# Squared tiles of two norms added in pairs by accumulating transfers, in a streaming encoder step on one core

## The reference

```
def _rmsnorm(x, g):
    y = x32 * rsqrt(mean(x32 * x32, axis=-1) + EPS) * g
def _swiglu(u, w_in, w_out):
    h = u @ w_in;  a, b = h[..., :D_FF], h[..., D_FF:]
    return (silu(a) * b) @ w_out
...
x = x + 0.5 * _swiglu(_rmsnorm(x, norm_ffn1[i]), ...)
x = x + mixer(_rmsnorm(x, norm_mix[i]))
x = x + 0.5 * _swiglu(_rmsnorm(x, norm_ffn2[i]), ...)
```

## Time and profile before

| what | value |
|---|---|
| time, median of 3 runs | 1911.73 us (1911.7 to 1914.8) |
| the profiled execution: own time | 1912.83 us |
| its span | 1911.0 us |
| TensorE busy | 1879.5 us, 98% |
| VectorE, ACT, POOL busy | 66%, 45%, 18% |
| share of the DMA engines' span: q1, q0 | 28.4%, 22.4% |

### The profile page before, as it was taken

One profiled execution on the slowest core, in us unless ns is written; L12 is line 12 of the kernel. 1 busy time (PEld: TensorE's weight loads), 2 busy tenths in 40 slices (PEclk: granted clock), 3 DMA queues, 4 the chain that ended last, 5 costly groups with the idle time before them and its releaser, 6 DMA issues.

```text
span 1911.0 us, 34429 instructions
## 1 busy us (share of the span) xinstructions
PE 1879.5 (98%) x13850; PEld 1856.6 (97%) x13850; DVE 1262.6 (66%) x1997; ACT 864.2 (45%) x1510; POOL 344.1 (18%) x361
## 2 busy tenths in 40 slices
PE   7999999998999999999999999999999999999998
PEld 7999999998999999999999999999989999999998
DVE  7884488667884488678853885462546988448843
ACT  6552355346652355345532553232434555235532
POOL 2220122121220122132201221200001522012112
PEclk9999999999999999999999999999999999999999
DMA  7763576433763577347644763222113476347632
GB/s 193 168 146 104 122 166 146 112 86 81 171 146 103 123 163 151 107 103 163 147 127 109 165 134 100 88 95 67 56 45 105 102 172 152 106 116 167 132 92 80
DMA packets 116830, 234.71 MB, mean 123 GB/s; under 512 B 13184, under 2 KB 15248, under 8 KB 116672
## 3 DMA queue, kind: packets, MB, share of 16 engines
q1 hardware_dynamic: 77440, 160.59, 28.4%
q0 software_dynamic: 38208, 69.42, 22.4%
q10 hardware_dynamic: 1024, 2.49, 0.3%
HBM read 228.92 MB, written 3.53 MB: 122 GB/s over the span
## 4 chain that ended last, share of the span: by engine, by line
PE 91%; DVE 4%; ACT 2%; DMA 2%; issue 1%; POOL 0%; DVEq 0%; ACTq 0%
PE ps L1774 48%; PE ps L1764 39%; DMA raw_y<-in_ffn_in 1%; DVE u L1234 1%; DVE w_lo L1180 1%; ACT w_hi L706 1%; PE ps L2086 0%; PE ps L2147 0%; PE ps L2089 0%; PE ps L1956 0%; PE ps L2076 0%; DMA x<-in_x 0%; ACT u L748 0%; PE ps L2061 0%; PE ps L2050 0%
## 5 line engine op out<-in xcount | busy, mean ns | idle before, releaser
L1774 PE MATMUL ps<-u,w_hi 128*128 128x288 f32 x4928 | 993.7, 297 | 18.1 <-DVE w_lo L1180 5.5
L1774 PEld LDWEIGHTS ps<-u,w_hi 128*128 128x128 f32 x4928 | 796.2, 189 | 23.6 <-DVE w_lo L1180 13.0
L1774 PE MATMUL ps<-u,w_lo 128*128 128x288 f32 x2464 | 730.9, 297 | 0.0
L1774 PEld LDWEIGHTS ps<-u,w_lo 128*128 128x128 f32 x2464 | 465.4, 189 | 0.0
L1764 PE MATMUL ps<-h_hi,w_hi 128*128 128x288 f32 x1386 | 298.0, 296 | 0.0
L1764 PE MATMUL ps<-h_hi,w_lo 128*128 128x288 f32 x1386 | 298.0, 296 | 0.0
L1764 PE MATMUL ps<-h_lo,w_hi 128*128 128x288 f32 x1386 | 297.9, 296 | 0.0
L706 ACT ACTIVATE w_hi<-w_raw 128x768 fp32r<-128x768 f32 (+3 forms) x164 | 136.0, 837 | 327.4 <-PE ps L1764 255.3
L1180 DVE TENSOR_TENSOR w_lo<-w_raw,w_hi 128x768 fp32r<-128x768 f32 (+3 forms) x164 | 168.7, 1037 | 165.4 <-ACT w_hi L706 163.2
L1764 PEld LDWEIGHTS ps<-h_hi,w_lo 128*128 128x128 f32 x1386 | 223.1, 189 | 0.0
L1764 PEld LDWEIGHTS ps<-h_hi,w_hi 128*128 128x128 f32 x1386 | 222.9, 189 | 0.0
(11 more groups left out here) (258 smaller groups left out, 2143.5 us busy)
## 6 DMA issues: line engine op xcount, KB each, us to landing
raw_a<-in_ffn_in SPq DMA_DIRECT2D x132, 256.0 KB, 3.8
w_raw<-in_ffn_out SPq DMA_DIRECT2D x64, 384.0 KB, 3.2
raw_y<-in_ffn_in SPq DMA_DIRECT2D x88, 256.0 KB, 3.5
raw_x<-in_ffn_in SPq DMA_DIRECT2D x88, 256.0 KB, 2.7
raw_x<-in_ffn_in POOLq DMA_DIRECT2D x88, 256.0 KB, 6.2
raw_y<-in_ffn_in POOLq DMA_DIRECT2D x88, 256.0 KB, 4.9
raw_z<-in_ffn_in POOLq DMA_DIRECT2D x88, 256.0 KB, 4.9
w_raw<-in_ffn_out SPq DMA_DIRECT2D x64, 320.0 KB, 3.0
```

The source lines that it names most:

```text
L1774: mm = pe.matmul(dst, w, m, start=prod in ("M1", "M2", "M5") and kp == 0 and p == 0, stop=kp == KP - 1 and p == 2, skip_group_check=prod i ...
```

## The change

ACT squares all eight tiles as before. Behind it, POOL issues transfers from SBUF to SBUF that add one squared tile of 288 KB to another within `sq8`, and TensorE multiplies the sums. In FFN a three sums are made (2 on 0, 3 on 1, 7 on 5) and tiles 0, 4, 6, 1, 5 are multiplied; in FFN b four sums (1 on 0, 3 on 2, 5 on 4, 7 on 6) and tiles 0, 2, 4, 6. In FFN a three tiles stand ahead of the group of M6, in FFN b two behind the second step of M1. In both, the last two tiles stand behind the last step of M6 instead of one behind each step. TensorE waits for a semaphore of each sum. POOL issues the last two sums of an FFN between `add_s4` of pair 1 and `add_s1` of pair 3.

```diff
+    sq8_summed = [sem(f"sq8_summed{s}") for s in range(4)]
...
+            def sum_squares(f, s, count):
+                to, of = ((0, 2), (1, 3), (5, 7))[s] if f is ffn_a else ((0, 1), (2, 3), (4, 5), (6, 7))[s]
+                pool.wait_ge(sq8_made, DT * f.i + count)
+                pool.dma_start(sq8[:, to, :], sq8[:, of, :], accum_op=ALU.add).then_inc(sq8_summed[s], 16)
...
                 add_s4(f, ph, 1)
+                if ph == 0 and f is ffn_a:
+                    sum_squares(f, 1, 6)
+                    sum_squares(f, 2, 8)
+                elif ph == 0 and f is ffn_b:
+                    sum_squares(f, 2, 6)
+                    sum_squares(f, 3, 8)
                 add_s1(f, ph, 3)
...
             add_s3_first(ffn_a, 0)
+            sum_squares(ffn_a, 0, 2)
...
             add_s3_first(ffn_b, 0)
+            sum_squares(ffn_b, 0, 2)
+            sum_squares(ffn_b, 1, 4)
...
             def norm_tiles(f, turns):
+                tiles = (0, 4, 6, 1, 5) if f is ffn_a else (0, 2, 4, 6)
                 for i in turns:
-                    j = (0, 2, 4, 6, 1, 3, 5, 7)[i] if f is ffn_a else i
-                    pe.wait_ge(sq8_made, DT * f.i + i + 1)
+                    if f is ffn_a and i in (1, 2):
+                        pe.wait_ge(sq8_made, i + 2)
+                    elif f is ffn_a:
+                        pe.wait_ge(sq8_summed[max(0, i - 2)], 16)
+                    else:
+                        pe.wait_ge(sq8_summed[i], 16 * (2 if i < 3 else 1))
...
-                            norm_tiles(f, range(4))
+                            norm_tiles(f, range(3))
...
-                        if order is COLD and products[0] == ("M6", 0):
-                            norm_tiles(f, (4 + kp,))
+                        if order is COLD and products[0] == ("M6", 0) and kp == KP - 1:
+                            norm_tiles(f, (3, 4) if f is ffn_a else (2, 3))
...
                             pe.wait_ge(x_ready, 2 * DT + 6)
-                            norm_tiles(f, range(4))
+                            norm_tiles(f, range(2))
```

More of the change, by code:

```diff
@@ L1813, in norm_tiles @@
             def norm_tiles(f, turns):
+                tiles = (0, 4, 6, 1, 5) if f is ffn_a else (0, 2, 4, 6)
                 for i in turns:
-                    j = (0, 2, 4, 6, 1, 3, 5, 7)[i] if f is ffn_a else i
-                    pe.wait_ge(sq8_made, DT * f.i + i + 1)
+                    if f is ffn_a and i in (1, 2):
[4 more added lines that the diff above has]
+                        pe.wait_ge(sq8_summed[i], 16 * (2 if i < 3 else 1))
+                    last = i == len(tiles) - 1
                     for h in range(2):
-                        mm = pe.matmul(ps[:, 6 + h, 0:HALF], mean_w[:, :], sq8[:, j, h * HALF:(h + 1) * HALF],
-                                       start=i == 0, stop=i == DT - 1, skip_group_check=True)
-                    if i == DT - 1:
+                        mm = pe.matmul(ps[:, 6 + h, 0:HALF], mean_w[:, :], sq8[:, tiles[i], h * HALF:(h + 1) * HALF],
+                                       start=i == 0, stop=last, skip_group_check=True)
+                    if last:
                         mm.then_inc(norm_psum, 1)
```

## The result

The changed kernel takes 1919.37 us (median of 14 runs), the kernel before 1914.16 us in 14 runs of the same comparison. The ratio is 1.0028, 95% interval 1.0015 to 1.004: slower by 5.4 us, interval 2.9 to 7.7. The forecast was 6.3 us more, 1918.0. The profiled execution took 1920.15 us for a span of 1918.3. In both kernels a few executions are some 6 us longer than the others (4 of 14 before, at 1920.3 to 1922.5, and 3 of 14 after, at 1925.2 to 1926.0); neither trace is of such a one.

A forecast was written before the change was run, and what follows sets the result against it. TensorE was 98% busy, but ACT's or DVE's queue ended the waits beside the removed tiles. Removal 0, early sums 0, late sums +3.0 and +3.3 made +6.3 us on the median 1911.73: 1918.0, range 1911.5 to 1922.

The forecast's parts named there:

- What the removal is worth: Both FFNs: 7.1 us of TensorE work removed ahead of waits that ACT's or DVE's queue ends; gain 0.
- (a): Early sums, both FFNs: they land before TensorE's next wait ends, or a later wait covers them; cost 0.
- The step that gave FFN a's landing, 26 to 27.5: First FFN: early sum issued at about 21.7 lands by about 26 to 27.5, before three tiles must start at 28.3.
- my bound of 3.8: Second FFN's early sum: least landing time, 3.8 us, taken from accumulating weight loads of 256 KB.
- (b) First FFN: Late sums fill the DMA engines and delay raw_y about 3 us, with it ACT and M7: +3.0 us.
- ACT stays the bound there: First FFN: late tiles end at 43.8, before ACT's root at 45, so ACT's lateness sets M7.
- (b) Second FFN: Late sums delay M7 through raw_y and through late tiles at half clock; +3.3 us, bounds 0 and +6.
- raw_y 4.2 us later: Second FFN: two late sums take all DMA engines 4.2 us ahead of raw_y, putting M7 at 474.3.
- my other step: Second FFN: sums land at 471.0 and 473.1, half-clock tiles end at 475.1; M7 +5.0, up to 1.7 given back.
- The price of a sum: Late sums cost the DMA engines what accumulating HBM loads do: 0.185 and 0.14 MB/us, 3.2 and 4.2 us for two.
- The estimate from the fit of the Trainium skill: 2.0 us plus bytes at 436 GB/s, 2.7 us per sum: late sums land early and the change costs nothing.
- Fair sharing: Rival, first FFN: queues share, raw_y only about 1 us late, sums finish at 42.9; +2.9, counted in the forecast's 0.55.

The follow-up runs named there:

- early_sums: Against the kernel before: only the early sums (one in FFN a, two in FFN b), late tiles multiplied one by one inside M6; ratio 1.0002, 0.4 us.
- dve_adds: Against the kernel before: two late sums per FFN made by DVE without transfers, early tiles multiplied one by one; ratio 0.9997, -0.6 us.
- traffic_probe: Against the kernel before: all eight tiles on TensorE, plus two unused accumulating transfers per FFN where the late sums stand; ratio 1.003, 5.7 us.
- late_sums: Against the kernel before: only the two late sums per FFN by transfer, early tiles multiplied one by one; ratio 1.0023, 4.4 us.
- pool_adds: The changed kernel with all seven sums made by POOL additions instead of transfers; against the kernel before, ratio 1.0025, 4.8 us.

## Why the prediction was right

- *What the removal is worth: 0.* `early_sums` (1.0002, three tiles less) and `dve_adds` (0.9997, four tiles less) show no gain.
- *(a) The early sums cost 0.* Right in sum: `early_sums` shows no cost, to within its interval of -2.3 to +3.1 us. The step that gave FFN a's landing, 26 to 27.5, was wrong: the sum shared the engines with two accumulating loads and SP's load and took 6.6 us, the tiles met the half clock, and M6 started 1.7 us late. It did not move raw_y: SP issued it 16.5 us behind M5 as before (34.15 - 17.62 and 34.08 - 17.55). In FFN b the lone sum landed after 3.3 us, under my bound of 3.8.
- *(b) First FFN, +3.0.* Measured +3.2, in one execution. The mechanism named is there: raw_y landed after 6.8 to 7.9 us in five traces with late sums in transfers, 7.4 on average, and after 4.8 on average in the six without; 2.6 us for about 3 forecast, and 3.3 between the two traces that the prediction compares. The distances say it less sharply: +2.2 to +3.9 us in those five traces, -0.5 to +2.8 in the four experiments at the time of the kernel before. `traffic_probe` shows that the traffic alone suffices. But "ACT stays the bound there" did not hold in the changed kernel's trace: the tiles ended at 45.43 and not at 43.8 (the first sum landed at 40.9 and not at 39.8, and the two tiles took 4.48 us and not 4.0), and M7 of pair 0 waited for them and not for ACT. The two paths end within about half a microsecond of each other, so the sum came out the same by either.
- *(b) Second FFN, +3.3.* Measured +2.1, in one execution. The step "raw_y 4.2 us later" was wrong: raw_y took 5.1 to 6.5 us in the five traces with late sums in transfers, 6.0 before, and 4.7 to 6.3 in five other traces without them, so no delay of it shows. In the changed kernel the two queues shared the engines (41.3% for q1 in 469 to 473, when it had 2.4% in the four us before); why q1 got through sooner here than in FFN a stays open. What cost was my other step, TensorE waiting for its own sums and the tiles at half clock: M7 3.5 us later than the lag of FFN a alone would put it, where I had 5.0, less some 1.4 because M7 no longer runs at half clock. `traffic_probe` (+0.5) beside `late_sums` (+2.4) shows this split, one execution each.
- *The price of a sum.* 0.16 to 0.18 MB/us against the 0.14 to 0.185 taken from loads out of HBM: the bet on which the size rested held. The estimate from the fit of the Trainium skill (DMA: Bandwidth & Descriptors, Anatomy of one DMA), 2.7 us, is near to a lone sum (3.3 us) and far from one in the full queue (up to 10.1 us).
- *Fair sharing.* Neither picture holds throughout: q1 moved nothing in 33 to 37 and had 28.9% in 37 to 41 (FFN a). The 3.05 us of q0's rest in that rival follow from no row shown.

The total is the firm part, +6.3 forecast and +5.4 (2.9 to 7.7) measured. Its split into +3.2 and +2.1 rests on one trace, and FFN a's distance moved by up to 3.3 us between kernels of the same time. That the first term came out within 0.2 us is luck.

## What to carry to other kernels

A busy share of 98% says little of one place: ask of each removed instruction what ends the next wait behind it. Here two ways of taking four tiles off TensorE without new traffic changed nothing or made it slower. An accumulating transfer cost the DMA engines twice the time of a plain load per byte here (0.16 to 0.185 against 0.375 MB/us), so it lands soon where the queues are empty (3.3 us) and can hold up an unrelated weight where they are full. When a wait is removed and the time stays, look for the same time further down before calling the experiment void: the chain through the weights of pair 2 showed itself only when ACT's order was changed.

## What the runs showed of the hardware

POOL's addition of two SBUF tiles held a DVE instruction of 1.05 us for 5.14 us. A transfer of one size, issued on one queue, landed after 3.3 to 10.1 us in the changed kernel, by what else was in flight. A plain load of 256 KB landed after 2.6 us with the accumulating queue empty (`pool_adds`) and after 6.8 to 7.9 us behind its backlog. TensorE's clock was at half behind an idle time of 1.97 us in FFN a of the changed kernel and stayed at full level behind one of 1.33 us. The idle time alone does not tell the level: behind one of 2.59 us ahead of M7 in FFN a of `early_sums` it read 1.00 in each window from 41 to 45.
